# Softplus in one activation, and activation tables loaded by written-out instructions, in a two-model transformer kernel

## The chip, the cores and the metric

The kernel runs on one core of a Trainium2 chip. A core has TensorE (PE, matrix products), VectorE (DVE), ScalarE (ACT, activation functions by table), GpSimd (POOL) and SyncE (SP, which here issues the DMAs). The metric is the time of one execution on the device in microseconds (us); lower is better. Inputs, weights and output are float32 in HBM.

## The reference

Two models of two layers each run one after the other on x of 256 tokens by 1024. The first has a Fourier and convolution mixer, a windowed attention and two mixtures of experts. The second has, in each of its two layers, a SwiGLU feed-forward block, a mixer of three attentions (stick-breaking, MLA, NSA) and a second feed-forward block. What the change touches is the stick-breaking attention:

```python
z = jnp.einsum('bqhd,bkhd->...', qb, k).astype(jnp.float32) * scale
strict = kpos[None, :] < qpos[:, None]
log_one_minus = jnp.where(strict, -jax.nn.softplus(z), 0.0)
suffix = lax.cumsum(log_one_minus, axis=3, reverse=True) - log_one_minus
w = jnp.where(strict, jnp.exp(jax.nn.log_sigmoid(z) + suffix), 0.0)
o = jnp.einsum('bhqk,bkhd->bqhd', w, v)
```

softplus(z) is ln(1 + e^z), which is also max(z, 0) + ln(1 + e^-|z|). The rest that it touches is where ACT changes its table: RMS norm (square, sqrt) ahead of every block, SiLU in the feed-forward blocks and experts, the layer norm of the convolution (sqrt, then SiLU), the router's softmax (exp), and the sigmoids of the gates.

## The kernel before

Every engine has its own program, written out by hand as one function (tensor_program, scalar_program, vector_program, ...). Each runs its instructions strictly in order; between engines they wait on semaphores, in the code as events (E.sb_z, E.sb_pe, ...). All ACT operations go through the helper af in line 1314, all products through mm in line 671 and all turns (transposes) through tp in line 675, so the profile gives these lines for most operations. On DVE, line 1690 is a tensor-tensor operation, 1698 one with a scalar between two tensors, 1701 a copy, 1695 and 1694 a tensor with scalars.

Matrix products that need float32 accuracy are done in three products of a high and a low part: ACT copies the weights or activations to a rounded high part ("cut"), DVE subtracts to get the low part, PE multiplies. The weights come through a ring of 12 slots, of which 6 are lent out as working space (lent_r, ring) in the mixers and feed-forward blocks.

Eleven normalisations, number 0 to 10, run by normalise(u) on ACT and DVE: ACT squares token tile 0 with a running sum, DVE tile 1; DVE makes the mean (line 1695), ACT takes Sqrt of both, DVE the reciprocal (1753), ACT scales tile 0 and DVE tile 1, and PE turns the result. Numbers 5, 7, 8 and 10 stand ahead of the feed-forward blocks; there ACT goes on with the cut of half a weight tile and eight high-part copies of the turned activations, and DVE with the low parts; PE's products wait for these. Numbers 6 and 9 stand ahead of the mixers, 4 and 5 follow one another.

In a mixer, stage A weaves three streams on each engine in a fixed ratio: stick_breaking (eight heads in four pairs, n = 0 to 3), mla_prepare (norms, rotations and turns of the MLA heads) and fillers, products of hT with weights of w_in (128x512, four records of the trace to a step) that are not needed until later. For each pair n, PE makes the logits of two heads in PSUM banks 0 and 1 (128 keys on the partitions, 384 columns each), ACT and DVE make mx.sp = softplus(z) there, DVE masks it, PE adds up the suffix with triangular matrices in banks 2 and 3 and makes the logits of pair n+1, DVE adds the mask and writes mx.z, ACT takes the exponential in place, and PE multiplies it with the values ("pv"). Of softplus, ACT takes Abs, Exp(-x) and Ln(x + 1), each in place in mx.z, and DVE one operation max(z, 0) + mx.z.

ACT's functions come from tables. An instruction ACT_TABLE_LOAD changes the set; in the kernel before none is written in the code. The compiler puts one ahead of each function that the loaded set lacks. The wait on a semaphore is a part of the function's own instruction, so such a load stands ahead of the wait. Copy, Identity, Square and Abs need no change of table.

Of the kernel before, what the change touches and what calls it, by code (L numbers as in the profile page):

```python
# [15 lines left out]
P = 128  # L16
# [180 lines left out]
def build(nc, A, consts, n_col, n_row):  # L197
# [147 lines left out]
    mx = Space()  # L345
# [42 lines left out]
    class E:  # L388
# [87 lines left out]
                                  [("z", 0)] + [(s, m) for n in range(4) for s, m in (("suffix", n), ("z", n + 1), ("pv", n)) if m < 4]])  # L476
    E.sb_ln, E.sb_w = Event(nc, "sb_ln", keys(2, 4)), Event(nc, "sb_w", keys(2, 4))
    E.sb_sp, E.sb_add = Event(nc, "sb_softplus", keys(2, 4)), Event(nc, "sb_add", keys(2, 4))
# [833 lines left out]
    def scalar_program():  # L1312
# [37 lines left out]

        def normalise(u):
            if u:
                C.wait_ge(*E.x_new.at(u - 1))
            af(xn[:, 0, :], x[:, 0, :], ACT.Square, accum_out=stat[:, 0:1]).then_inc(*act.ev(E.norm_act, u, "sq"))
            C.wait_ge(*E.norm_dve.at(u, "mean"))
            af(stat[:, 2:4], stat[:, 2:4], ACT.Sqrt).then_inc(*act.ev(E.norm_act, u, "sqrt"))
            C.wait_ge(*E.norm_dve.at(u, "r"))
            af(xn[:, 0, :], x[:, 0, :], ACT.Copy, scale=stat[:, 4:5]).then_inc(*act.ev(E.norm_act, u, "x0"))

        def shifted_hT(u, mod_cols):  # L1360
# [13 lines left out]
        def fourier(ahead):  # L1374
# [25 lines left out]
            for _ in range(CONV_STEPS[0]):  # L1400
                next(ahead)
            C.wait_ge(*E.fc_dve.at(("var", 0)))
            af(fc.rstd, fc.rstd, ACT.Sqrt).then_inc(*act.ev(E.fc_act, ("std", 0)))
            C.wait_ge(*E.fc_dve.at(("norm", 0)))
            for ch in range(4):
# [9 lines left out]
        def experts(layer, ahead):  # L1415
            m, u = moe[layer], norm_of_moe[layer]
            normalise(u)
            for k in range(1, KT, 2):
                C.wait_ge(*E.hT_pe.at(u, k))
                C.wait_ge(*E.norm_dve.at(u, "r"))  # L1420
                af(hT[:, k, :], psum[:, k % 4, 0:S], ACT.Identity, scale=gain_col[:, k:k + 1],
                   bias=mods[1][:, k:k + 1]).then_inc(*act.ev(E.hT_act, u, k))
            C.wait_ge(*E.rt_dve.at(layer, "max"))
            af(m.aff, m.aff, ACT.Exp).then_inc(*act.ev(E.rt_act, layer, "exp"))
# [6 lines left out]
            for k in range(KT):  # L1431
                if k >= KT - ROUTER_STEPS[2]:
                    next(ahead, None)
                if k % 2:
                    C.wait_ge(*E.rt_pe.at(layer, ("gather", k)))
                    af(m.xg[:, 0:N_GRP, k, :], psum[:, k % 4, :].rearrange("p (g c) -> p g c", g=N_GRP), ACT.Identity,
                       scale=gain_col[:, k:k + 1], bias=mods[1][:, k:k + 1]).then_inc(*act.ev(E.rt_act, layer, ("xg", k)))
            run(ahead)
            for g in range(N_GRP):
                if g:  # L1440
                    C.wait_ge(*E.moe_dve.at(layer, g - 1, ("hid", 1)))
                C.wait_ge(*E.moe_mm.at(layer, g, "gate", 3, 3))
                for n in range(2):
                    half = slice(n * 512, (n + 1) * 512)
                    af(m.gated[:, half], psum[:, n, :], ACT.Silu).then_inc(*act.ev(E.moe_act, layer, g, ("silu", n)))
                C.wait_ge(*E.moe_mm.at(layer, g, "down", 3, 3))
                af(m.y[:, 0:512], psum[:, 6, :], ACT.Copy).then_inc(*act.ev(E.moe_act, layer, g, ("y", 0)))
# [78 lines left out]
        def stick_breaking(l):  # L1526
            for n in range(4):
                if n:
                    C.wait_ge(*E.sb_pe.at(l, "pv", n - 1))
                C.wait_ge(*E.sb_pe.at(l, "z", n))  # L1530
                af(mx.z, psum[:, 0:2, 0:3 * P], ACT.Abs).then_inc(*act.ev(E.sb_z, l, n))
                C.wait_ge(*act.now)
                af(mx.z, mx.z, ACT.Exp, scale=-1.0).then_inc(*act.own())
                C.wait_ge(*act.now)
                af(mx.z, mx.z, ACT.Ln, bias=1.0).then_inc(*act.ev(E.sb_ln, l, n))
                yield
                yield
                C.wait_ge(*E.sb_add.at(l, n))
                af(mx.z, mx.z, ACT.Exp).then_inc(*act.ev(E.sb_w, l, n))
                yield  # L1540

# [63 lines left out]
        def mixer(l):  # L1605
# [13 lines left out]
            for i2, (c0, width) in enumerate(mi_tokens):  # L1619
# [3 lines left out]
                dst = (mx.sv, mx.low)[i2][:, 1, :]  # L1623
                af(dst, psum[:, 2 * i2 + 1, 0:width], ACT.Copy).then_inc(*act.ev(E.mi_act, l, ("t", i2)))
            C.wait_ge(*E.mi_pe.at(l, "gates"))
            af(mx.gates, psum[:, 4, 0:48].rearrange("p (t n) -> p t n", t=TT), ACT.Sigmoid).then_inc(*act.ev(E.mi_act, l, "gates"))
# [27 lines left out]
            weave(fill, STEPS_C, (attention(nsa_units, 12 + 12 * l, bufs=mx.bufs), 1))  # L1654
            run(fill)
            cut("mo", l, 0, 0)
            for br in range(3):
# [30 lines left out]
    def vector_program():  # L1688
# [415 lines left out]
        def stick_breaking(l):  # L2104
            for n in range(4):
                yield
                V.wait_ge(*E.sb_ln.at(l, n))
                alone(stt(mx.sp, psum[:, 0:2, 0:3 * P], 0.0, mx.z, ALU.max, ALU.add))
                tt(mx.sp, mx.sp, wide(K("strict"), 2), ALU.mult).then_inc(*dve.ev(E.sb_sp, l, n))
                yield  # L2110
                V.wait_ge(*E.sb_pe.at(l, "suffix", n))
                tt(mx.z, psum[:, 2:4, 0:3 * P], wide(K("strict_add"), 2), ALU.add).then_inc(*dve.ev(E.sb_add, l, n))
                yield
# [291 lines left out]
```

## Time and profile before

| | us |
|---|---|
| median of 3 runs | 3107.53 |
| lowest, highest | 3103.37, 3108.70 |
| the profiled execution | 3107.78 |
| its span in the trace | 3106.4 |

In that execution PE is busy 2498.5 us (80% of the span), DVE 1141.0 us (37%), ACT 815.9 us (26%) and POOL 3.2 us. The mean clock granted to PE is 0.882 of full speed. The page also follows the chain of work that ended last back from the final instruction, and the trace lists single instructions in order of time. Times of an instruction are its start from the start of the span and its duration; idle time of its engine just before it stands in brackets, with what ended it. A granted clock of 1.00 is 2.4 GHz, 0.50 is 1.2 GHz.

### The profile page before, as it was taken

The numbers are of one execution on the slowest core, as the hardware profiler recorded it, in microseconds if no ns is written. First come the engines' busy times: TensorE is split into PE (matmuls) and PEld (weight loads), VectorE is DVE, ScalarE is ACT, GpSimd is POOL, SyncE is SP. The second block draws the span as 40 slices with busy tenths as digits, with TensorE's granted clock in tenths as the row PEclk, the third lists the DMA queues.
The fourth block names the chain that finished last, engine by engine and source line by source line (L and its number), as shares of the span: only waits on it lengthen the run. The fifth ranks groups of instructions, "written<-read, shape, count | busy, mean of one in ns | idle before, by whom it ended". The sixth has DMA issues, their size and how long they took to land.

```text
span 3106.4 us, 31572 instructions
## 1 busy us (share of the span) xinstructions
PE 2498.5 (80%) x13586; PEld 1587.9 (51%) x13586; DVE 1141.0 (37%) x1682; ACT 815.9 (26%) x1161; POOL 3.2 (0%) x7
## 2 busy tenths in 40 slices
PE   5877666667776666666998887889999998888899
PEld 2643111113552111113988453579989774545897
DVE  1732100103542100103545525465455543356554
ACT  2231000002240000002433332544444333224443
POOL 0000000000000000000000000000000000000000
PEclk9878888888877888888999888899999997899999
DMA  8468999997436999998654223246556432234463
GB/s 307 172 235 343 409 409 409 409 409 288 174 139 256 409 409 409 409 409 283 181 189 132 68 69 109 95 136 185 186 159 188 151 108 68 71 120 129 134 185 109
DMA packets 396960, 703.66 MB, mean 227 GB/s; under 512 B 17171, under 2 KB 232339, under 8 KB 396694
## 3 DMA queue, kind: packets, MB, share of 16 engines
q1 hardware_dynamic: 396822, 701.65, 63.7%
q8 instruction: 107, 1.75, 0.2%
q14 instruction: 31, 0.25, 0.0%
HBM read 700.56 MB, written 1.05 MB: 226 GB/s over the span
## 4 chain that ended last, share of the span: by engine, by line
PE 57%; DMA 24%; DVE 9%; ACT 6%; SPq 3%; issue 1%; DVEq 0%; ACTq 0%
PE psum L671 55%; DMA ring<-in_moe_w_down 10%; DMA ring<-in_moe_w_up 8%; DMA ring<-in_moe_w_gate 6%; SPq L548 3%; PE psum L675 2%; DVE arena L1698 2%; ACT ring L1314 1%; DVE arena L1690 1%; ACT L1314 1%; ACT lent_r L1314 1%; DVE lent_r L1690 1%; ACT xn L1314 1%; ACT arena L1314 1%; DVE xn L1690 1%
## 5 line engine op out<-in xcount | busy, mean ns | idle before, releaser
L671 PE MATMUL psum<-ring,arena 128*32 128x512 f32 (+3 forms) x3672 | 691.3, 686 | 293.9 <-DMA ring<-in_moe_w_up 111.1
L671 PE MATMUL psum<-lent_r 128*128 128x256 f32 (+1 forms) x3440 | 635.8, 298 | 25.5 <-DVE lent_r L1690 25.4
L671 PEld LDWEIGHTS psum<-ring,arena 128*32 128x32 f32 (+2 forms) x3672 | 188.9, 133 | 800.2 <-issue 285.7
L671 PEld LDWEIGHTS psum<-lent_r 128*128 128x128 f32 x3440 | 549.1, 194 | 45.6 <-issue 26.5
L671 PE MATMUL psum<-arena_r,lent_r 128*128 128x256 f32 (+1 forms) x1888 | 521.8, 318 | 16.2 <-DVE arena_r L1690 8.6
L1690 DVE TENSOR_TENSOR lent_r<-ring,lent_r 128x2048 fp32r<-128x2048 f32 (+1 forms) x158 | 349.3, 2212 | 283.2 <-ACT lent_r L1314 283.2
L671 PEld LDWEIGHTS psum<-arena_r,lent_r 128*128 128x128 f32 x1888 | 369.0, 196 | 40.5 <-DVE arena_r L1690 10.6
L1314 ACT ACTIVATE arena<-psum 128x512 f32<-128x512 f32 (+3 forms) x126 | 61.9, 507 | 1173.4 <-PE psum L671 1107.7
L1314 ACT ACTIVATE lent_r<-ring 128x2048 fp32r<-128x2048 f32 (+1 forms) x158 | 289.7, 1838 | 169.9 <-PE psum L671 169.9
L671 PE MATMUL psum<-ring,hT 128*128 128x512 f32 (+2 forms) x640 | 286.8, 586 | 5.2 <-ACT arena L1314 2.7
L1701 DVE COPY arena<-psum 128x256 f32<-128x256 f32 (+6 forms) x130 | 66.0, 512 | 482.6 <-PE psum L671 353.0
L671 PE MATMUL psum<-lent_r,arena_r 128*128 128x512 f32 x1056 | 241.5, 390 | 0.4 <-DVE lent_r L1690 0.2
L1701 DVE COPY arena<-arena 128x256 f32<-128x256 f32 (+3 forms) x32 | 13.0, 410 | 579.7 <-PE psum L671 577.4
L671 PEld LDWEIGHTS psum<-lent_r,arena_r 128*128 128x128 f32 x1056 | 197.6, 188 | 42.9 <-issue 2.0
L1314 ACT ACTIVATE ring<-psum 128x256 f32<-128x256 f32 (+3 forms) x172 | 81.1, 479 | 436.2 <-PE psum L671 399.4
L1690 DVE TENSOR_TENSOR arena_r<-ring,arena_r 128x256 fp32r<-128x256 f32 (+2 forms) x130 | 125.0, 963 | 138.4 <-ACT arena_r L1314 138.4
L671 PEld LDWEIGHTS psum<-ring,hT 128*128 128x128 f32 x640 | 118.2, 216 | 105.4 <-issue 95.4
L1314 ACT ACTIVATE arena_r<-ring 128x256 fp32r<-128x256 f32 (+2 forms) x130 | 109.7, 846 | 106.0 <-PE psum L671 62.7
L671 PE MATMUL psum<-arena_r 128*128 128x256 f32 (+2 forms) x704 | 117.3, 322 | 6.5 <-DVE arena_r L1690 6.5
L675 PE MATMUL psum<-const_sb,arena 128*128 128x128 f32 (+4 forms) x326 | 55.5, 311 | 68.8 <-DVE arena L1690 50.4
L671 PEld LDWEIGHTS psum<-arena_r 128*128 128x128 f32 x704 | 103.9, 199 | 13.4 <-DVE arena_r L1690 4.7
L671 PE MATMUL psum<-arena 128*64 128x128 f32 (+7 forms) x576 | 92.1, 391 | 18.6 <-DVE arena L1701 10.1
(127 smaller groups left out, 1487.7 us busy)
## 6 DMA issues: line engine op xcount, KB each, us to landing
ring<-in_moe_w_gate SPq DMA_DIRECT2D x128, 1024.0 KB, 18.5
ring<-in_moe_w_up SPq DMA_DIRECT2D x128, 1024.0 KB, 18.6
ring<-in_moe_w_down SPq DMA_DIRECT2D x128, 1024.0 KB, 18.5
ring<-in_ffn_wi SPq DMA_DIRECT2D x176, 512.0 KB, 5.2
ring<-in_ada_w SPq DMA_DIRECT2D x48, 1024.0 KB, 7.9
ring<-in_w_in SPq DMA_DIRECT2D x46, 1024.0 KB, 5.1
ring<-in_ffn_wo SPq DMA_DIRECT2D x44, 1024.0 KB, 4.9
ring<-in_w_out SPq DMA_DIRECT2D x8, 1024.0 KB, 5.0
```

The source lines that it names most:

```text
L548: Y.dma_start(view(ring_sb[:, n, :]), src).then_inc(slot_sem[n], 16)
L671: return T.matmul(out, lhsT, rhs, start=start, stop=stop, **kw)
L675: return T.transpose(out, in_, ident[0:k, 0:k])
L1314: return C.activation(out, a, f, **kw)
L1690: return V.tensor_tensor(out, a, b, op)
L1698: return V.scalar_tensor_tensor(out, a, s, b, op0, op1)
L1701: return V.tensor_copy(out, a)
```

## The change

In stick-breaking, Abs, Exp and Ln on ACT and the max-and-add on DVE become one activation, Softplus, which reads the logits from PSUM and writes mx.sp; DVE's mask then works on it at once. Softplus waits for the previous pair's suffix product (which reads mx.sp) in place of its pv product, and the addition on DVE that writes mx.z now waits for that pv. Behind Softplus stands a written-out load of Exp's table, and behind each exponential but the last one of Softplus's.

In every normalisation a load of Sqrt's table is written ahead of Square, and ahead of the wait for x. In those ahead of the feed-forward blocks a load of Silu's table follows the scaled copy. Further written-out loads: Sqrt and Silu at the convolution's norm, Exp at the router, Silu ahead of the experts, Sigmoid ahead of the mixer's gates and ahead of the merge of its three branches. The compiler still adds loads where a set is lacking; there are 73 in all against 70.

```diff
         def normalise(u):
+            C.preload_act_table(ACT.Sqrt)
             if u:
                 C.wait_ge(*E.x_new.at(u - 1))
             af(xn[:, 0, :], x[:, 0, :], ACT.Square, accum_out=stat[:, 0:1]).then_inc(*act.ev(E.norm_act, u, "sq"))
...
             af(xn[:, 0, :], x[:, 0, :], ACT.Copy, scale=stat[:, 4:5]).then_inc(*act.ev(E.norm_act, u, "x0"))
+            if u in norm_of_ff:
+                C.preload_act_table(ACT.Silu)
...
+            C.preload_act_table(ACT.Sqrt)
             C.wait_ge(*E.fc_dve.at(("var", 0)))
             af(fc.rstd, fc.rstd, ACT.Sqrt).then_inc(*act.ev(E.fc_act, ("std", 0)))
+            C.preload_act_table(ACT.Silu)
...
+            C.preload_act_table(ACT.Exp)
             C.wait_ge(*E.rt_dve.at(layer, "max"))
...
             run(ahead)
+            C.preload_act_table(ACT.Silu)
...
         def stick_breaking(l):
             for n in range(4):
+                C.wait_ge(*E.sb_pe.at(l, "z", n))
                 if n:
-                    C.wait_ge(*E.sb_pe.at(l, "pv", n - 1))
-                C.wait_ge(*E.sb_pe.at(l, "z", n))
-                af(mx.z, psum[:, 0:2, 0:3 * P], ACT.Abs).then_inc(*act.ev(E.sb_z, l, n))
-                C.wait_ge(*act.now)
-                af(mx.z, mx.z, ACT.Exp, scale=-1.0).then_inc(*act.own())
-                C.wait_ge(*act.now)
-                af(mx.z, mx.z, ACT.Ln, bias=1.0).then_inc(*act.ev(E.sb_ln, l, n))
+                    C.wait_ge(*E.sb_pe.at(l, "suffix", n - 1))
+                af(mx.sp, psum[:, 0:2, 0:3 * P], ACT.Softplus).then_inc(*act.ev(E.sb_z, l, n))
+                C.preload_act_table(ACT.Exp)
                 yield
                 yield
                 C.wait_ge(*E.sb_add.at(l, n))
                 af(mx.z, mx.z, ACT.Exp).then_inc(*act.ev(E.sb_w, l, n))
+                if n < 3:
+                    C.preload_act_table(ACT.Softplus)
                 yield
...
+            C.preload_act_table(ACT.Sigmoid)
             C.wait_ge(*E.mi_pe.at(l, "gates"))
...
             run(fill)
+            C.preload_act_table(ACT.Sigmoid)
             cut("mo", l, 0, 0)
...
         def stick_breaking(l):
             for n in range(4):
                 yield
-                V.wait_ge(*E.sb_ln.at(l, n))
-                alone(stt(mx.sp, psum[:, 0:2, 0:3 * P], 0.0, mx.z, ALU.max, ALU.add))
+                V.wait_ge(*E.sb_z.at(l, n))
                 tt(mx.sp, mx.sp, wide(K("strict"), 2), ALU.mult).then_inc(*dve.ev(E.sb_sp, l, n))
                 yield
                 V.wait_ge(*E.sb_pe.at(l, "suffix", n))
+                if n:
+                    V.wait_ge(*E.sb_pe.at(l, "pv", n - 1))
                 tt(mx.z, psum[:, 2:4, 0:3 * P], wide(K("strict_add"), 2), ALU.add).then_inc(*dve.ev(E.sb_add, l, n))
```

The orders of PE, POOL and SP stay as they are. On ACT, at pair n=2 of the first mixer (ring<-psum 128x768 is the read of the logits, arena or ring<-psum 128x512 the copy of a filler product; L1539 and L1545 are the two written-out loads in stick_breaking):

```order
 L1314 ACTIVATE arena<-psum 96x256 x3
 L1314 ACTIVATE arena<-psum 128x512
 L1314 ACTIVATE ring<-psum 128x768
-L1314 ACTIVATE ring<-ring 128x768
-L1314 ACT_TABLE_LOAD
-L1314 ACTIVATE ring<-ring 128x768
+L1539 ACT_TABLE_LOAD
 L1314 ACTIVATE arena<-psum 96x256
```

Two activations and the load between them leave, and a load for the exponential stands behind the Softplus; n=3 is built alike.

On ACT, from normalisation 4 to the first feed-forward block (xn,stat<-x is Square, stat<-stat Sqrt, xn<-x,stat the scaled copy, lent_r<-psum,col_sb the eight high-part copies, lent_r<-ring the cuts):

```order
+L1352 ACT_TABLE_LOAD
+L1314 ACTIVATE xn,stat<-x 128x1024
+L1314 ACTIVATE stat<-stat 128x2
+L1314 ACTIVATE xn<-x,stat 128x1024
+L1361 ACT_TABLE_LOAD
 L1314 ACTIVATE lent_r<-ring 128x1024
 L1314 ACTIVATE lent_r<-psum,col_sb 128x256 x8
 L1314 ACTIVATE lent_r<-ring 128x1024
 L1314 ACTIVATE lent_r<-ring 128x2048
-L1314 ACT_TABLE_LOAD
 L1314 ACTIVATE ring<-psum 128x256
```

Sqrt's load passes Square and the wait for x, and Silu's load passes three cuts and the eight copies.

On DVE, pair n=2 of the first mixer before (ring<-psum,ring is max-and-add, ring<-ring,const_sb the mask, ring<-psum,const_sb the sum into mx.z, arena<-psum 96x256 the copy of a turned MLA head):

```order
526 L1701 COPY arena<-psum 128x256 [waits s_sb_pe]
527 L1701 COPY arena<-psum 96x256 [waits s_mla_pe]
528 L1698 SCALAR_TENSOR_TENSOR ring<-psum,ring 128x768 [waits s_sb_ln]
529 L1690 TENSOR_TENSOR ring<-ring,const_sb 128x768 [waits s_own_dve]
530 L1690 TENSOR_TENSOR ring<-psum,const_sb 128x768 [waits s_sb_pe]
531 L1701 COPY arena<-psum 128x256 [waits s_sb_pe]
```

and after (lines are numbered anew):

```order
524 L1709 COPY arena<-psum 128x256 [waits s_sb_pe]
525 L1709 COPY arena<-psum 96x256 [waits s_mla_pe]
526 L1698 TENSOR_TENSOR ring<-ring,const_sb 128x768 [waits s_sb_z]
527 L1698 TENSOR_TENSOR ring<-psum,const_sb 128x768 [waits s_sb_pe]
528 L1709 COPY arena<-psum 128x256 [waits s_sb_pe]
529 L1698 TENSOR_TENSOR ring<-ring,const_sb 128x768 [waits s_sb_z]
```

The max-and-add is gone and the mask waits for ACT's Softplus itself; the copy ahead of it stays ahead.

## Rows read from the trace of the kernel before

**Rows 1.** The page: the chain that ended last, shares of the span.
```profile
PE 57%; DMA 24%; DVE 9%; ACT 6%; SPq 3%; issue 1%; DVEq 0%; ACTq 0%
```

**Rows 2.** ACT's groups: count | busy us, mean ns | idle before, releaser.
```profile
L1314 ACT ACT_TABLE_LOAD x70 | 89.8, 1283 | 14.8 <-DVE stat L2333 13.5
...
L1314 ACT ACTIVATE ring<-ring 128x768 f32<-128x768 f32 x24 | 20.2, 843 | 54.5 <-DVE ring L1690 54.1
```

**Rows 3.** Waits of PE, 1700 to 1850 us: total, times, longest.
```profile
PE psum L671 <- DVE ring L1690: 13.2, 4, 4.9
```

**Rows 4.** Timeline of ACT, n=3: start, duration [idle before].
```profile
1802.47 0.81 ACT L1314 ACTIVATE ring<-psum 128x768 f32<-128x768 f32 x1
1803.30 0.84 ACT L1314 ACTIVATE ring<-ring 128x768 f32<-128x768 f32 x1
1804.16 1.28 ACT L1314 ACT_TABLE_LOAD   x1
1805.46 0.84 ACT L1314 ACTIVATE ring<-ring 128x768 f32<-128x768 f32 x1
```

**Rows 5.** Timeline of DVE, n=2 (a copy) and n=3.
```profile
1788.28 0.42 DVE L1701 COPY arena<-psum 96x256 f32<-96x256 f32 x1 [4.08 <-PE psum L675]
...
1806.33 0.96 DVE L1698 SCALAR_TENSOR_TENSOR ring<-psum,ring 128x768 f32<-128x768 f32 x1 [5.83 <-ACT ring L1314]
1807.32 0.96 DVE L1690 TENSOR_TENSOR ring<-ring,const_sb 128x768 f32<-128x768 f32 x1
```

**Rows 6.** Timeline of PE, stage A of the first mixer (hT: fillers).
```profile
1732.20 0.70 PE L671 MATMUL psum<-ring 64*128 64x256 f32 x2 [3.05 <-DVE ring L1690]
...
1763.83 0.92 PE L671 MATMUL psum<-ring 64*128 64x256 f32 x2 [4.88 <-DVE ring L1690]
...
1788.29 1.88 PE L671 MATMUL psum<-ring,hT 128*128 128x512 f32 x4
1791.75 0.70 PE L671 MATMUL psum<-ring 64*128 64x256 f32 x2 [1.57 <-DVE ring L1690]
...
1796.37 0.93 PE L671 MATMUL psum<-ring 64*128 64x256 f32 x8
1797.23 1.98 PE L671 MATMUL psum<-ring,hT 128*128 128x512 f32 x4
...
1802.62 1.98 PE L671 MATMUL psum<-ring,hT 128*128 128x512 f32 x4 [0.69 <-ACT arena L1314]
1808.34 1.06 PE L671 MATMUL psum<-ring 64*128 64x256 f32 x2 [3.73 <-DVE ring L1690]
...
1816.38 3.08 PE L671 MATMUL psum<-ring,hT 128*128 128x512 f32 x4
```

**Rows 7.** Timeline of PE, n=2 in the second mixer.
```profile
2615.97 0.70 PE L671 MATMUL psum<-ring 64*128 64x256 f32 x2 [1.58 <-DVE ring L1690]
...
2624.63 3.51 PE L671 MATMUL psum<-ring,hT 128*128 128x512 f32 x4
```

**Rows 8.** Stretches: length, PE busy (count), granted clock, DMA share, GB/s.
```profile
1792.00:1796.00 4.00, 4.00 (x19) 1.00 0.00 0
...
2618.00:2622.00 4.00, 4.00 (x11) 0.50 0.00 0
```

**Rows 9.** Timeline of all engines, normalisation 7: mean, Sqrt, cut.
```profile
2076.47 0.17 DVE L1695 TENSOR_SCALAR stat<-stat 128x2 f32<-128x2 f32 x1
...
2077.67 0.20 ACT L1314 ACTIVATE stat<-stat 128x2 f32<-128x2 f32 x1
...
2079.16 1.04 ACT L1314 ACTIVATE lent_r<-ring 128x1024 fp32r<-128x1024 f32 x1
```

**Rows 10.** ACT: the group of Squares, and that of normalisation 1.
```profile
L1314 ACT ACTIVATE xn<-x 128x1024 f32<-128x1024 f32 x11 | 11.6, 1055 | 74.9 <-DVE x L1690 46.0 <-DVE x L1698 28.9
...
216.08 1.05 ACT L1314 ACTIVATE xn<-x 128x1024 f32<-128x1024 f32 x1
```

**Rows 11.** Timeline of ACT, Sigmoid's load at the first mixer's merge.
```profile
2001.60 1.28 ACT L1314 ACT_TABLE_LOAD   x1
```

More of the change, by code:

```diff
@@ L476, in build @@
                                   [("z", 0)] + [(s, m) for n in range(4) for s, m in (("suffix", n), ("z", n + 1), ("pv", n)) if m < 4]])
-    E.sb_ln, E.sb_w = Event(nc, "sb_ln", keys(2, 4)), Event(nc, "sb_w", keys(2, 4))
+    E.sb_w = Event(nc, "sb_w", keys(2, 4))
     E.sb_sp, E.sb_add = Event(nc, "sb_softplus", keys(2, 4)), Event(nc, "sb_add", keys(2, 4))
```

## Prediction

> **What bounds the kernel now.** I read the chain of work that ended last first: TensorE (PE) has 57% of it, weight transfers 24%, VectorE (DVE) 9% and ScalarE (ACT) 6% [rows 1]. So an ACT edit can only pay where PE waits for ACT, or for a DVE operation that ACT held up. Grouping ACT's instructions shows what is edited: 70 table loads of 1283 ns, and the in-place Exp and Ln on a 128x768 tile at 843 ns [rows 2]. The idle time ahead of these 70 loads is 14.8 us, 13.5 of it at the program's start: a load that the compiler placed sits right behind the previous ACT instruction and ahead of the wait of its user, so it already runs in ACT's idle time wherever there is any. Writing such a load out by hand gains nothing by itself; it pays only if it passes an instruction that is on the path.
>
> Two kinds of place are on the path. First the stick-breaking stage (stage A of each mixer, four head pairs n = 0 to 3, two layers). There PE waits 13.2 us in four waits for DVE's masked softplus [rows 3]: 3.05, 4.88, 1.57 and 3.73 us, and as much again in the second layer. Second the eleven normalisations, where the load of Sqrt stands between Square and Sqrt.
>
> **Stick-breaking, step by step.** For n=3 the old chain is a Copy of the filler product, Abs 0.80, Exp 0.84, load 1.28, Ln 0.84 [rows 4], then DVE's max-and-add and the mask, 0.99 us apart [rows 5], then PE. The new chain is Softplus and the mask. Softplus reads the same 128x768 of PSUM as Abs; no row shows it, so I bound it by Abs (0.80) and Ln (0.84) and take 0.80, since the functions in the rows differ only by where they read. Its own table is loaded behind the preceding exponential, which ended 4 us earlier, so the load is covered; without that cover it would cost 1.28. Removed from ACT and DVE: 0.84 + 1.28 + 0.84 + 0.99 = 3.95 us for each pair. PE takes only what it was waiting for, because it is filled with other products:
> - n=3: Softplus from 1802.47 to 1803.28, mask to 1804.27. PE is busy with a filler until 1802.62 + 1.98 = 1804.60 [rows 6]. The wait of 3.73 goes, gain 3.8.
> - n=2: the mask stands in DVE's queue behind the copy of a turned MLA key head that ends at 1788.70 [rows 5]; it would be done at 1789.7. PE's filler ends at 1788.29 + 1.88 = 1790.17, and PE restarted at 1791.75 [rows 6]. Gain 1.6.
> - n=0 and n=1: DVE comes to this pair only after long MLA work (squares and sums), so ACT's part is hidden anyway and what goes is the 0.99 us of max-and-add. For n=1 ACT's copies of turned heads also come about 1.7 us sooner (Exp and Ln gone, the load stays as that of Exp), of which PE's fillers leave 0.2. Gains 1.0 and 1.2; waits of about 2.1 and 3.9 us remain.
>
> That is 7.6 us a layer and 15.3 in both. The new DVE wait (the sum into mx.z waits for the previous pair's last product) and ACT's new wait for the previous suffix are for work finished at least 10 us earlier: nothing. The wasted loads (Exp behind Softplus when a Sqrt comes between, three more in all, 73 for 70) lie in ACT's idle time; if all three were exposed they would cost 3.8.
>
> **The clock behind those waits.** Suffix product and filler after n=2 in the first layer run at the high clock (2.4 GHz): PE starts at 1791.75, has the suffix done by 1796.37, and the filler takes 1.98. After n=3, behind a wait of 3.73, they run at the low one (1.2 GHz): 1808.34 to 1816.38 and 3.08 [rows 6]. In the second layer n=2 falls too: the same stretch that took 5.48 (1791.75 to 1797.23) takes 8.66 and its filler 3.51 [rows 7]; the granted clock is 0.50 there and 1.00 at n=2 of the first layer [rows 8]. If PE no longer stops ahead of n=2 and n=3, I expect both to stay high, as n=2 in the first layer did after 1.57 us: (8.04 - 4.62) + (3.08 - 1.98) = 4.5 for n=3 in each layer and 3.18 + 1.53 = 4.7 for n=2 in the second, 13.7 us together. The bounds are 0 (the clock falls all the same) and, if n=0 with its wait cut from 3.05 to 2.1 also stays high, another 4.7 or so in each layer, 23 in all. I take the middle: two of the three kinds of row have no wait left, n=0 keeps most of its own.
>
> **Normalisations.** In number 7, DVE's mean starts at 2076.47 and takes 0.17; Sqrt starts only at 2077.67, behind the load [rows 9]. With the load ahead of Square, in idle time (ACT waits 74.9 us in all ahead of the Squares [rows 10], in nine of the eleven), Sqrt starts at 2076.67: gain 1.0. It is the same for 6, 8, 9 and 10; in 2, 3 and 4 DVE's square is later and leaves 0.7, 0.9 and 0.9. Number 5 had no load (Sqrt's table is still in). In numbers 0 and 1 ACT goes from a Copy straight to Square, as number 1's row shows [rows 10], nothing covers the load, and Sqrt also waits for the mean behind it: +0.4 each. Against that, ahead of the four feed-forward blocks (5, 7, 8, 10) Silu's load now comes directly behind the scaled copy of x, ahead of the cut at 2079.16 and the eight high-part copies, through which the chain runs: +1.28 each. Before, that load lay behind them where PE was still multiplying. Sum: -5.0 - 2.5 + 0.8 + 5.1 = -1.6 us. Sigmoid's load at the merge moves from behind three copies to ahead of them in one unbroken run of ACT work [rows 11]: nothing. All other written-out loads stand where the compiler's did.
>
> The Trainium skill (ScalarE: Activation LUTs, What ACT_TABLE_LOAD costs) puts a switch at 1.28 for the load and about 1.38 for a drain. The trace disagrees: the next instruction starts 0.01 us behind the 1.28 [rows 4]. By the page the normalisations would come to about -2.5 instead of -1.6, the rest unchanged. The same page (Table sets: the hidden batching unit) advises to do all of one set before switching, which speaks against alternating Softplus and Exp. By it the eight pairs would lose up to a load each; the rows of ACT's idle time say the loads are covered.
>
> **Sum.** -15.3 - 13.7 - 1.6 = -30.6 us on the profiled execution of 3107.78 (span 3106.4), which lies 0.25 above the median of 3107.53: 3077 us.
>
> **Rivals.**
> 1. The clock falls all the same, or at other places in its stead. For: the second layer's n=2 fell after a wait of only 1.58 us. Against: n=2 of the first layer. Then -16.9: 3091. With one or two of the three stretches, 3082 to 3087.
> 2. The clock also stays high at n=0, in one or both layers: 3072 or 3067.
> 3. PE's fillers absorb more than I find, or loads of Softplus come out exposed ahead of their user, 1.28 in each of six places: about 3098 to 3103, near no change. Against it are the ends of the fillers, read above.
> 4. The loads do not move at all: then only the arithmetic counts and it is -15.3 with or without the clock, 3079 or 3092; inside the range.
> 5. Slower. Softplus is evaluated in several passes and takes D instead of 0.80. Its slack is 0.3 us at n=3, 2.4 at n=2, 1.1 at n=1 and over 10 at n=0, so it costs 3D - 6.2 a layer, and the waits return and with them the low clock. It turns the sign at D = 4.9 us, six times Abs; at 6 us the time would be 3114. Nothing in the rows shows a function that costs more than another.
>
> **Chances.** Forecast (3073 to 3081) 0.42; rival 2 0.17; rival 1 0.30; rival 3 0.06; rival 5 and anything else that makes it slower 0.05. The range takes in the forecast and rivals 1 and 2 but for their far ends: 3066 to 3094. Faster by over 0.2% (6 us, about what a measurement tells from no change) 0.91; within it 0.05; slower 0.04.
>
> **What would show it.** In stage A no ACT work but Softplus between a filler's Copy and DVE's mask; PE's waits for the softplus down from 13.2 us to about 6 a layer, at n=0 and n=1 alone; suffix products of n=2 and n=3 at 4.6 us each. In normalisation 7 Sqrt right behind the mean, and the cut a load later behind the scaled copy. It is wrong if Softplus takes over 1.1 us, if ACT stands at a load while DVE or PE waits for it, or if the granted clock in n=2 and n=3 is at 0.5.

## The result, and the profile after

| | before | after |
|---|---|---|
| median, us | 3108.11 | 3078.55 |
| lowest, highest | 3103.37, 3112.18 | 3076.59, 3084.10 |
| the profiled execution | 3107.78 | 3084.10 |
| its span | 3106.4 | 3082.8 |

The ratio of the times is 0.9908, with a 95% interval of 0.9889 to 0.9927: 29.6 us less. 3077 had been forecast. The profiled execution of after is the slowest of its four, so its trace shows a loss of 23.6 us in the span and not of 30; two further runs of the same kernel, with traces of their own, serve beside it below (the repeats of after). Before has four runs here, three in the table ahead of the change.

The page of after, first the busy time and then the chain that ended last, by engine (before: [rows 1]):

```profile
PE 2435.6 (79%) x13586; PEld 1573.0 (51%) x13586; DVE 1133.7 (37%) x1674; ACT 807.9 (26%) x1148; POOL 3.2 (0%) x7
...
PE 57%; DMA 26%; DVE 9%; ACT 5%; SPq 2%; issue 1%; DVEq 0%; ACTq 0%
```

ACT and DVE are busy only 8.0 and 7.3 us less; PE, with the same 13586 products, 62.9 us less, which fits the granted clock (0.882 before, 0.917 now). Most of that lies in the products of the experts, as their group in the page of after shows (count | busy us, mean ns | idle before, releaser):

```profile
L671 PE MATMUL psum<-ring,arena 128*32 128x512 f32 (+3 forms) x3672 | 646.1, 618 | 339.6 <-DMA ring<-in_moe_w_up 129.4
```

Before, the group was busy 691.3 us and idle 293.9: what the clock gave there, 45.2 us, went into waiting for weights, 45.7 us more. So the mean clock of a whole run is no measure of the gain: the two repeats of after have 0.919 and 0.900 at spans of 3075.9 and 3074.2 us.

The waits of PE in stage A of the first mixer of after, 1690 to 1840 us: total, times, longest (before: [rows 3], 13.2 us in four waits).

```profile
PE psum L671 <- DVE ring L1698: 5.9, 2, 3.8
```

The timeline of ACT at n=3 (before: [rows 4]): start, duration, operation, in brackets the idle time ahead and what ended it.

```profile
1798.73 0.81 ACT L1314 ACTIVATE ring<-psum 128x768 f32<-128x768 f32 x1
1799.56 1.28 ACT L1539 ACT_TABLE_LOAD   x1
```

The first row is Softplus. It takes 0.81 us, as Abs did in [rows 4], and no load stands ahead of it.

The timeline of PE in the same stage (before: [rows 6]). The pairs of 64x256 products open the suffix products of n=0, 1, 2 and 3; hT marks fillers.

```profile
1730.24 1.09 PE L671 MATMUL psum<-ring 64*128 64x256 f32 x2 [2.06 <-DVE ring L1698]
...
1762.39 1.22 PE L671 MATMUL psum<-ring 64*128 64x256 f32 x2 [3.85 <-DVE ring L1698]
...
1788.02 0.70 PE L671 MATMUL psum<-ring 64*128 64x256 f32 x2
...
1793.50 1.98 PE L671 MATMUL psum<-ring,hT 128*128 128x512 f32 x4
...
1798.89 1.98 PE L671 MATMUL psum<-ring,hT 128*128 128x512 f32 x4 [0.69 <-ACT arena L1314]
1800.80 0.70 PE L671 MATMUL psum<-ring 64*128 64x256 f32 x2
```

At n=2 and n=3 the wait is gone and the pair takes 0.70 us, which is the high clock; at n=0 and n=1 waits of 2.06 and 3.85 us remain, and the pair takes 1.09 and 1.22.

Normalisation 7, timeline of DVE (the mean) and ACT (before: [rows 9]):

```profile
2065.91 0.17 DVE L1703 TENSOR_SCALAR stat<-stat 128x2 f32<-128x2 f32 x1
...
2066.12 0.20 ACT L1314 ACTIVATE stat<-stat 128x2 f32<-128x2 f32 x1 [0.32 <-DVE stat L1703]
2066.55 1.15 ACT L1314 ACTIVATE xn<-x,stat 128x1024 f32<-128x1024 f32 x1 [0.23 <-DVE stat L1761]
2067.72 1.28 ACT L1361 ACT_TABLE_LOAD   x1
2069.01 1.06 ACT L1314 ACTIVATE lent_r<-ring 128x1024 fp32r<-128x1024 f32 x1
```

Sqrt now starts 0.21 us behind the start of the mean (before 1.20), and the cut 2.46 us behind that of the scaled copy, since Silu's load stands between them.

Because PE's instructions are the same in both kernels, they can be laid side by side one by one. How much shorter (-) or longer (+) a stretch between two of them is than in before; the first column gives its bounds on before's clock, and a normalisation's stretch starts with the last product ahead of it:

| stretch, us | after | first repeat of after | second repeat |
|---|---|---|---|
| norms 4 and 5 and first products, 1439 to 1480 | +0.5 | +0.4 | +0.4 |
| stage A, first mixer, 1700 to 1840 | -11.4 | -15.3 | -15.3 |
| norm 7 and first products, 2074 to 2100 | +0.6 | +1.7 | +1.7 |
| norm 8 and first products, 2272 to 2300 | +0.2 | +0.8 | +0.9 |
| stage A, second mixer, 2530 to 2670 | -14.9 | -15.9 | -15.9 |
| norm 10 and first products, 2903 to 2960 | +0.1 | +1.3 | +1.3 |
| whole span | -23.6 | -30.5 | -32.2 |

The gain is that of the two stages A. It was forecast at 12.1 and 16.9 there.

### The profile page after: what moved, and what is told of

Its sections match the earlier page's. It is cut to its first block, busy times and chain, and to the rows that moved or that the text cites. A ratio compares the mean times of both kernels' runs of the same rounds, so it can differ in the third digit from the quotient of the medians.

```text
span 3082.8 us, 31557 instructions
## 1 busy us (share of the span) xinstructions
PE 2435.6 (79%) x13586; PEld 1573.0 (51%) x13586; DVE 1133.7 (37%) x1674; ACT 807.9 (26%) x1148; POOL 3.2 (0%) x7
## 4 chain that ended last, share of the span: by engine, by line
PE 57%; DMA 26%; DVE 9%; ACT 5%; SPq 2%; issue 1%; DVEq 0%; ACTq 0%
PE psum L671 55%; DMA ring<-in_moe_w_up 10%; DMA ring<-in_moe_w_down 8%; DMA ring<-in_moe_w_gate 7%; PE psum L675 2%; SPq L548 2%; DVE arena L1706 2%; DVE arena L1698 2%; ACT ring L1314 1%; ACT lent_r L1314 1%; DVE lent_r L1698 1%; ACT arena L1314 1%; DVE arena L1709 1%; DVE xn L1698 1%; DVE arena_r L1698 1%
## 5 line engine op out<-in xcount | busy, mean ns | idle before, releaser
L671 PE MATMUL psum<-ring,arena 128*32 128x512 f32 (+3 forms) x3672 | 646.1, 618 | 339.6 <-DMA ring<-in_moe_w_up 129.4
L671 PE MATMUL psum<-lent_r 128*128 128x256 f32 (+1 forms) x3440 | 637.2, 299 | 25.7 <-DVE lent_r L1698 25.7
```

What stands on the lines that cost most here:

```text
L671: return T.matmul(out, lhsT, rhs, start=start, stop=stop, **kw)
```

## The experiments

Each run of a set stands beside runs of the kernel before on the same chip (medians 3110.59, 3108.01 and 3107.96 in the three sets). The sets ran on different chips, so across sets the ratios are to be compared, not the times.

**Which half of the change does it.** One kernel has the stick-breaking part alone, the other the written-out loads alone. The first drops these lines from after, and the five further loads outside stick-breaking likewise:

```diff
         def normalise(u):
-            C.preload_act_table(ACT.Sqrt)
...
-            if u in norm_of_ff:
-                C.preload_act_table(ACT.Silu)
```

> The changed kernel without its written-out loads outside stick-breaking: the compiler places those again (Sqrt's behind Square, Silu's behind the cuts). My theory puts nearly the whole gain into stick-breaking, about 26 us by the trace of the changed kernel (11.3 in the first mixer, 14.5 in the second), and the moved loads at -1.6: this kernel at 3080 +- 3 us, Sqrt of normalisation 7 again 1.0 us later, cut 1.28 earlier relative to the scaled copy. The rival, that the loads carry the gain, expects over 3095.

Measured: 3076.47 us (3075.44 to 3077.29), ratio 0.9892 [0.9877, 0.9907], 0.5 below the 3080 +- 3 expected and far from the rival.

The second keeps all those loads and puts the old softplus back:

```diff
-                af(mx.sp, psum[:, 0:2, 0:3 * P], ACT.Softplus).then_inc(*act.ev(E.sb_z, l, n))
-                C.preload_act_table(ACT.Exp)
+                af(mx.z, psum[:, 0:2, 0:3 * P], ACT.Abs).then_inc(*act.ev(E.sb_z, l, n))
+                C.wait_ge(*act.now)
+                af(mx.z, mx.z, ACT.Exp, scale=-1.0).then_inc(*act.own())
+                C.wait_ge(*act.now)
+                af(mx.z, mx.z, ACT.Ln, bias=1.0).then_inc(*act.ev(E.sb_ln, l, n))
```

> The other part alone: all written-out loads outside stick-breaking, with Abs, Exp, Ln and max-and-add as before. My theory: -1.6 us, 3106 +- 3, not to be told from no change. The rival: 3095 or below. A second rival, that the Silu load in front of the cuts costs more than the 1.28 counted, expects over 3110.

Measured: 3109.15 us (3106.23 to 3114.64), ratio 1.0 [0.9992, 1.0009], at the upper end of the 3106 +- 3 expected. The whole gain is stick-breaking's, and the loads together are worth nothing that can be measured. That is a sum of a gain and a cost, though, as the next kernel shows.

The trace of this second kernel holds a lesson on the clock. Its instructions at n=2 of the first mixer, and their wait, are those of before, but the timeline of PE reads:

```profile
1786.12 0.70 PE L671 MATMUL psum<-ring 64*128 64x256 f32 x2 [1.58 <-DVE ring L1699]
1788.99 1.22 PE L671 MATMUL psum<-ring 64*128 64x256 f32 x2
1793.16 1.66 PE L671 MATMUL psum<-ring 64*128 64x256 f32 x8
```

In before the eight products behind the same wait took 0.93 us [rows 6], here 1.66: the clock falls during the suffix. After a wait of 1.6 us it may fall or not with the same instructions around it, which is also what [rows 6] against [rows 7] showed.

**Silu's load.** After without the load of Silu in the four normalisations ahead of the feed-forward blocks:

```diff
-            if u in norm_of_ff:
-                C.preload_act_table(ACT.Silu)
```

> The changed kernel without the written-out load of Silu in the four normalisations ahead of the feed-forward blocks; the compiler places it again behind the cuts. My theory: the cut in normalisation 7 starts 1.28 us sooner behind the scaled copy, and so do PE's first products, 5.1 us in all: 3073.5 +- 3. The rival, that PE or DVE would be late there anyway, expects the time of the changed kernel, 3078.5.

Measured: 3069.07 us (3066.52 to 3071.96), ratio 0.9869 [0.9856, 0.9882]. That is 4.4 below the 3073.5 expected and 9.5 below after as measured in its own set (12 by the ratios), more than four loads. But in the same set it is also 7.4 us below the kernel with stick-breaking alone (3076.47, with no overlap of the runs), from which it differs by the written-out loads other than Silu's in the normalisations. The prediction had put -6.7 on that difference, all of it Sqrt's. So Sqrt's loads do gain, and Silu's give it back. The kernel was run again, together with after.

> The changed kernel once more, as one corner of a two by two square: Silu's load written out or not, and the masks of n=0 and n=1 as they are or earlier. 3073 to 3079.

> The changed kernel without Silu's load in the four normalisations. If the first run's gain is real (a load of 1.28 us on the path in each of four places, plus a little), it is 5 to 8 us below the changed kernel of the same set; if that was the spread between chips and runs, 0 to 3.

Measured: after 3074.08 us (3071.56 to 3079.51), ratio 0.9892 [0.9875, 0.991]; without Silu's load 3069.23 us (3068.27 to 3070.05), ratio 0.9874 [0.9859, 0.9889]. The difference is 4.9 us, near the 5.1 of four loads and at the lower end of the 5 to 8 expected. Timeline of PE in normalisation 10, first of before, then of after's second repeat, then of the kernel without Silu's load; the rows are the two groups of turns.

```profile
2908.37 1.97 PE L675 MATMUL psum<-const_sb,xn 128*128 128x128 f32 x8 [4.86 <-ACT xn L1314]
2910.97 1.97 PE L675 MATMUL psum<-const_sb,xn 128*128 128x128 f32 x8 [0.64 <-DVE arena_r L1698]
```

```profile
2873.91 1.97 PE L675 MATMUL psum<-const_sb,xn 128*128 128x128 f32 x8 [3.87 <-ACT xn L1314]
2877.94 1.97 PE L675 MATMUL psum<-const_sb,xn 128*128 128x128 f32 x8 [2.06 <-DVE arena_r L1706]
```

```profile
2870.67 1.97 PE L675 MATMUL psum<-const_sb,xn 128*128 128x128 f32 x8 [3.87 <-ACT xn L1314]
2873.27 1.97 PE L675 MATMUL psum<-const_sb,xn 128*128 128x128 f32 x8 [0.64 <-DVE arena_r L1704]
```

Both effects reach PE. Sqrt's load ahead of Square takes 0.99 us off the wait for the first turns, and Silu's load puts 1.42 us on the wait for the second, since DVE's low parts there wait for what ACT does behind the load. It is the same 1.42 in normalisations 5, 7 and 8. Over the stretches of the table above, the kernel without Silu's load has -1.8, -0.2, -0.2 and -1.0 us at normalisations 5, 7, 8 and 10, where after's second repeat has +0.4, +1.7, +0.9 and +1.3: 7.5 us in all, 5.7 of them the four waits, the rest products that run at the low clock for longer behind them.

The two profiled spans differ by 5.5 us and not by 7.5, because the clock also falls at other places that the edit doesn't touch. Without the load stage A of the second mixer is 3.0 us shorter than in the repeat (-18.9 against -15.9), stage A of the first 2.8 us longer (-12.5 against -15.3), and the turns and products just ahead of normalisation 7 take 2.5 us more. Timeline of PE at n=0 of the second mixer, after's second repeat first:

```profile
2540.11 0.70 PE L671 MATMUL psum<-ring 64*128 64x256 f32 x2 [2.06 <-DVE ring L1698]
2542.42 1.17 PE L671 MATMUL psum<-ring 64*128 64x256 f32 x2
2546.54 1.66 PE L671 MATMUL psum<-ring 64*128 64x256 f32 x8
```

```profile
2540.00 0.70 PE L671 MATMUL psum<-ring 64*128 64x256 f32 x2 [2.06 <-DVE ring L1696]
2542.31 0.70 PE L671 MATMUL psum<-ring 64*128 64x256 f32 x2
2544.62 0.93 PE L671 MATMUL psum<-ring 64*128 64x256 f32 x8
```

The same wait of 2.06 us stands ahead of both. In one the clock falls within the suffix, in the other it stays high throughout, which is rival 2 of the prediction in one place. The profiled run of after lost it at once (1730.24 above, 1.09 us), which accounts for most of its 4 us more in the first mixer.

**Does a wait that PE gets back cost more than its length?** Four more reads of the logits ahead of Softplus at n=2 and n=3 hold it up; their results are overwritten by it.

```diff
+                if n >= 2:
+                    for _ in range(4):
+                        af(mx.sp, psum[:, 0:2, 0:3 * P], ACT.Abs).then_inc(*act.own())
+                        C.wait_ge(*act.now)
                 af(mx.sp, psum[:, 0:2, 0:3 * P], ACT.Softplus).then_inc(*act.ev(E.sb_z, l, n))
```

> The changed kernel with four Abs (0.80 us each, 3.3 us together) put ahead of Softplus at n=2 and n=3, into the same tile, so that PE's waits come back there in part: about 0.9 us at n=2 and 3.0 at n=3, in both mixers, 7.8 us by their lengths. If a wait also brings the low clock with it, as I reckoned, suffix and filler behind n=3 (and perhaps n=2) cost 4.5 us more each: 17 to 26 us in all, 3095 to 3104. If the clock gain has another cause, only the 7.8: 3086.

Measured: 3112.08 us (3107.44 to 3121.84), ratio 1.0015 [1.0004, 1.0026]: 33.5 above after (33 by the ratios), beyond the range expected. The timeline of ACT at n=2 and that of PE show why:

```profile
1776.90 3.33 ACT L1314 ACTIVATE ring<-psum 128x768 f32<-128x768 f32 x4
1780.26 1.28 ACT L1314 ACT_TABLE_LOAD   x1
```

```profile
1783.40 0.86 PE L671 MATMUL psum<-ring 64*128 64x256 f32 x2 [3.62 <-DVE ring L1702]
...
1808.29 1.22 PE L671 MATMUL psum<-ring 64*128 64x256 f32 x2 [5.78 <-DVE ring L1702]
```

The text ahead of the prediction has Abs among the functions that need no change of table, since it needed none in the kernel before. Beside Softplus it does: the compiler put a load ahead of the four and another behind them, 2.56 us more in each pair than meant, and the waits that came back are 3.62 and 5.78 us in each mixer, 18.8 in both. The other 14.7 us I put down to the clock and what follows from it; the next kernel tests that. (The Trainium skill, ScalarE: Activation LUTs, Table sets: the hidden batching unit, lists abs among the cheap functions of every set; the loads of this trace say otherwise for the set that is loaded for Softplus.)

The same with Copy, which needs no load:

```diff
-                        af(mx.sp, psum[:, 0:2, 0:3 * P], ACT.Abs).then_inc(*act.own())
+                        af(mx.sp, psum[:, 0:2, 0:3 * P], ACT.Copy).then_inc(*act.own())
```

> The changed kernel once more, beside the others on one chip. 3078 +- 3 us.

> As the run with four Abs ahead of Softplus at n=2 and n=3, but with four Copies, for which Softplus's table serves (Abs brought two loads of 1.28 with it and waits of 3.6 and 5.8 us, 18.8 in both mixers, at a price of 33.5). Waits of 0.9 at n=2 and 3.0 at n=3, 7.8 us in all. If the low clock comes with a wait, 4.5 more at n=3 in each mixer, and at n=2 where it falls there: 17 to 26 us above the changed kernel; 7.8 if not.

Measured: after 3073.45 us (3068.82 to 3077.26), ratio 0.9889 [0.9875, 0.9904]; with the Copies 3094.37 us (3089.78 to 3099.44), ratio 0.9957 [0.9944, 0.997]. After is 1.6 below the 3078 +- 3 expected of it. The price of the Copies is 20.9 us, within the 17 to 26. PE's waits for the softplus, 1685 to 1830 us of the kernel with the Copies, and its timeline at n=2 and n=3:

```profile
PE psum L671 <- DVE ring L1702: 9.9, 4, 3.9
```

```profile
1785.73 0.70 PE L671 MATMUL psum<-ring 64*128 64x256 f32 x2 [0.92 <-DVE ring L1702]
1788.04 0.70 PE L671 MATMUL psum<-ring 64*128 64x256 f32 x2
1790.35 0.93 PE L671 MATMUL psum<-ring 64*128 64x256 f32 x8
...
1801.66 0.70 PE L671 MATMUL psum<-ring 64*128 64x256 f32 x2 [3.08 <-DVE ring L1702]
1805.02 1.22 PE L671 MATMUL psum<-ring 64*128 64x256 f32 x2
1809.06 3.62 PE L671 MATMUL psum<-ring,hT 128*128 128x512 f32 x4
```

Waits of 0.92 and 3.08 us came back, 8.0 in both mixers, at a price of 20.9. After 0.92 the clock stays high; after 3.08 it falls in the middle of the suffix, and the filler behind it takes 3.62 us in place of 1.98. By the traces the two stages A together are 17.3 us longer than in the first repeat of after: 7.6 of it PE's idle time, and 9.7 the same products taking longer, 9.3 of these behind n=3 (4.6 and 4.7, for the 4.5 expected). So the two parts of the forecast are both real. The last 3.6 of the 20.9 us lie outside these stages and aren't explained.

**The two waits that are left.** At n=0 and n=1 DVE comes to the mask late because of MLA work ahead of it. Here the mask of n=0 is moved ahead of the squares of the q norm, and that of n=1 ahead of the copy of the fifth turned q head:

```diff
+MASK_AT = {2: 0, 9: 1}
...
+        def mask(l, n):
+            V.wait_ge(*E.sb_z.at(l, n))
+            tt(mx.sp, mx.sp, wide(K("strict"), 2), ALU.mult).then_inc(*dve.ev(E.sb_sp, l, n))
...
-                V.wait_ge(*E.sb_z.at(l, n))
-                tt(mx.sp, mx.sp, wide(K("strict"), 2), ALU.mult).then_inc(*dve.ev(E.sb_sp, l, n))
+                if n >= 2:
+                    mask(l, n)
...
+            def mla_and_masks():
+                for step in itertools.count():
+                    if step in MASK_AT:
+                        mask(l, MASK_AT[step])
+                    if next(mla, mla) is mla:
+                        return
+                    yield
```

> The changed kernel with DVE's masks of n=0 and n=1 moved ahead in its queue: n=0 to before the squares of the q norm, n=1 to before the copy of the fifth turned q head, both behind Softplus's end in the trace. My theory (PE's wait and, behind it, the low clock set the price): the waits of 2.06 and 3.85 us go; the suffix and the fillers behind them run at the high clock, 8 us a layer at n=0 and, with DVE's norm of k becoming the bound, 4 to 6 at n=1: 24 to 28 us in all, 3050 to 3056. The rival, that only the waits count, expects 11.8: 3067. A third, that DVE's MLA work is the bound of stage A, so that moving a mask frees nothing, expects 3078.

Measured: 3051.27 us (3043.04 to 3053.34), ratio 0.9817 [0.9804, 0.983], 22.2 below after in the same set. PE's longest waits, 1685 to 1830 us, and its timeline from n=0 (the 128x256 rows are pv products, the 64x256 rows suffixes):

```profile
PE psum L672 <- ACT ring L1315: 4.8, 4, 2.8
```

```profile
1727.17 0.93 PE L672 MATMUL psum<-ring 64*128 64x256 f32 x8
...
1734.57 0.88 PE L672 MATMUL psum<-ring 128*64 128x256 f32 x8 [2.84 <-ACT ring L1315]
...
1744.48 0.70 PE L672 MATMUL psum<-ring 64*128 64x256 f32 x2
...
1755.15 0.88 PE L672 MATMUL psum<-ring 128*64 128x256 f32 x8 [1.50 <-ACT ring L1315]
```

The 5.9 us a mixer of waiting for the softplus are gone; all four suffixes run at 0.70 and 0.93 us. What is late next is the exponential, which pv waits for: 4.8 us in four waits, most of it there before (3.3 in after). In the profiled run of the third set, below, PE is idle 7.5 us less in the two stages than in after's second repeat (11.8 gone, part of it come back as waits for the exponential), and the same products take 16.5 us less, 11.6 of them at n=1. So most of the 22 us is the clock's. It is less than the 24 to 28 expected, as a difference.

**Everything at once.** Masks early, without Silu's load, and Sqrt's load written out only from normalisation 2 on (in 0 and 1 nothing covers it):

```diff
-            C.preload_act_table(ACT.Sqrt)
+            if u >= 2:
+                C.preload_act_table(ACT.Sqrt)
```

> The kernel with the early masks, without Silu's load ahead of the cuts, and without Sqrt's load ahead of Square in normalisations 0 and 1. My theory: another 5.1 + 0.8 us by the lengths of the loads (9 by the run without Silu's load): 3042 to 3050.

Measured: 3050.44 us (3044.91 to 3051.12), ratio 0.9812 [0.9799, 0.9825]. That is 0.4 above the 3042 to 3050 expected, and against 3051.27 in the same set no gain, where 5.9 had been expected. To see whether Silu's load counts at all on this base, the two were run without the change to Sqrt's load, beside after and after without Silu's load:

> The changed kernel with the masks of n=0 and n=1 earlier on DVE: 22 to 26 below the changed kernel of the same set, as in its first run.

> Both edits. The load and the masks lie in different stages, so if the two are independent it is as much below the kernel with the early masks as the version without Silu's load is below the changed kernel: 5 to 8 us, 3043 to 3046. If what a sooner start of the feed-forward products gives is taken back behind them (a clock that falls elsewhere), it is within 3 us of the kernel with the early masks.

Measured: masks early 3053.31 us (3052.98 to 3054.94), ratio 0.9824 [0.9809, 0.9839]; the same without Silu's load 3044.85 us (3042.39 to 3051.08), ratio 0.9795 [0.9779, 0.981]. With masks early the time is 20.8 us below after, where 22 to 26 had been expected; leaving out Silu's load as well takes off 8.5 more, just over the 5 to 8. The square of the third set:

| us | masks as in after | masks early |
|---|---|---|
| Silu's load written out | 3074.08 | 3053.31 |
| left to the compiler | 3069.23 | 3044.85 |

Both edits hold in both rows and columns, and the last kernel, 63 us under the kernel before, is the fastest by its median. The size of the small one stays uncertain, though: 4.9 and 8.5 here, 0.8 between the two kernels of the second set, and 2.5 between the profiled runs of the right column. There the four normalisations gain 7.1 us together; stage A, which differs in nothing, is 1.5 us shorter in the first mixer and 1.8 longer in the second, and between the first mixer's stage A and normalisation 7 it loses 3.7. Whether Sqrt's load in normalisations 0 and 1 matters can't be told from the times at that spread. In the traces PE's first turn of normalisation 1 comes 0.42 us later with the load than without.

## Why the prediction was right, point by point

**Softplus** takes 0.81 us, where 0.80 had been taken from Abs. Its load and that of Exp lie in ACT's idle time. Rival 5 (several passes) falls with this row, and rival 4 (the loads don't move) too.

**The waits.** Forecast: 13.2 us a layer down to about 6, with 2.1 and 3.9 left at n=0 and n=1. Measured: 5.9, with 2.06 and 3.85. The method was to end each wait at the later of DVE's mask and PE's filler; it was right to 0.1 us at all four pairs, and so rival 3 falls. PE's idle time ahead of and between the four suffixes falls by 1.0, 1.2, 1.6 and 3.7 us, for 1.0, 1.2, 1.6 and 3.8 forecast. Of 15.3 us in both layers 14.6 are left in the repeats, because a wait of 0.2 us for the exponential of n=3, which the prediction doesn't have, is new in each, and the rest is rounding.

**The clock.** Forecast -13.7, with bounds 0 and -23. The stages A are shorter by 26.3 us in the profiled run and by 31.2 in its repeats. PE's idle time there is 12.4 and 14.6 us less, so the same products take 13.8 and 16.6 us less. The time of PE's products, idle time left out, from one suffix to the next (for n=3 up to 1840 and 2670 us of before):

| us | before | after | both repeats | with the Copies |
|---|---|---|---|---|
| first mixer, n=0 | 23.7 | 25.5 | 20.8 | 20.8 |
| n=1 | 25.7 | 24.9 | 25.3 | 25.4 |
| n=2 | 12.2 | 12.1 | 12.1 | 12.2 |
| n=3 | 31.2 | 26.6 | 26.6 | 31.2 |
| second mixer, n=0 | 23.8 | 25.5 | 24.0 | 24.0 |
| n=1 | 24.4 | 25.0 | 25.1 | 25.2 |
| n=2 | 16.9 | 12.1 | 12.1 | 12.2 |
| n=3 | 32.0 | 27.3 | 27.3 | 32.0 |

The three stretches that the prediction named (n=3 twice, n=2 in the second mixer) gained 4.6, 4.7 and 4.8 us in all three traces of after, 14.1 for 13.7, and the Copies took n=3 back to what it was, behind a wait of 3.08 us; that shows the mechanism. Two things differ from the forecast in detail. First n=0 doesn't simply keep its state: with 2.06 us ahead of it, it ran fully at the high clock, fell in its middle, or fell at its start, from run to run, worth up to 4 us a mixer. Second, the prediction gave n=2 of the first layer no gain from the clock since in that one trace it ran high; the experiment with the loads alone found it low behind the same wait. Rows of one trace told the price of a fallen clock well, but not how often it falls. That before's one trace had n=2 high in one mixer and low in the other, and not twice low, is luck for the sum: with both low, as with the loads alone, it would have been 4.7 us more.

**Normalisations.** Forecast -1.6 for Sqrt's and Silu's loads together. The times agree with a sum near zero and can't tell its sign: stick-breaking alone has the ratio 0.9892, after 0.9908, 0.9889 and 0.9892 in its three sets, and the loads alone lie within 2.8 us up and 2.5 down. The two terms behind the sum were both right. Sqrt's loads were put at -6.7. Counted from the last product ahead of a normalisation, PE's first turn comes 0.99 us sooner than in before at numbers 6 to 10, 0.7 and 0.9 at 2 and 3, 0.9 for 4 (at the turns of 5), and 0.4 later at 1, in all three traces of after; with number 0, where 0.4 later is seen on ACT, that is the forecast term by term, and the time says 7.4 us in the first set. Silu's loads were put at +5.1; each costs PE 1.42 us and not 1.28, 5.7 in all, and the time says 4.9 on after. What the prediction lacked is that the products behind the turns start at the low clock and leave it sooner or later from run to run: at normalisation 7 the three traces have +0.6, +1.7 and +1.7 where the two terms give +0.4. The prediction's own signs didn't fit together, either: ACT standing at a load while DVE waits was to mean that it is wrong, and this is just what its term for Silu's load describes. (Of what the order ahead of the prediction marks as new there, Square, Sqrt and the scaled copy are in both kernels; ACT has 16 activations fewer and 3 loads more, 1148 rows for 1161.)

The Trainium skill's drain of about 1.38 us (ScalarE: Activation LUTs, What ACT_TABLE_LOAD costs) isn't there in after either: the cut follows the 1.28 us load of 2067.72 by 0.01 us. The -2.5 that the prediction worked out for it doesn't come out: with 1.38 us more for each moved load, an estimate, the eight normalisations that gain would gain 11.0 more and the four of Silu's load lose 5.5 more (at 0 and 1 the two cancel), -7.1. The Trainium skill's advice to do all of one set before switching (the same page, Table sets: the hidden batching unit) would have counted against the change; the alternation of Softplus and Exp cost nothing here, since the waits that are left are those worked out without any load in them.

**The sum** held because its parts did: 14.6 for 15.3 of waits, 13.8 to 16.6 for 13.7 of clock, and near zero for 1.6. The trace on record is 6.9 and 8.6 us longer than its siblings, 4.9 of it in the stages A, where n=0 fell at its start, so it alone would have suggested a miss that wasn't there.

## What to carry to other kernels

Removing a chain of small operations from ScalarE and VectorE pays only where TensorE waits for it, and there it may pay twice: 8.0 us of waits put back cost 20.9, because waits of 3 us let the clock fall under the products that follow (about half of it by the traces). End each wait by hand at the later of its producer and of TensorE's own fillers, and then look at which engine's queue holds the rest; here two masks moved ahead of other VectorE work brought 22 us, nearly as much as the whole change. Don't write out a table load that the compiler already places ahead of a wait, and never put one ahead of instructions that the next stage waits for (1.42 us at PE each). Do write one out where the compiler's stands inside a chain that TensorE waits for and there is idle time ahead of the chain: Sqrt's, moved ahead of Square, brought up to 0.99 us each. And start a comparison of a stretch at the last product ahead of the edit, or changes of the clock from elsewhere hide its effect.

## What the runs showed of the hardware

- Softplus over 128x768 from PSUM takes 0.81 us on ScalarE, as Abs and Copy do (3.33 us for four Abs, 4.17 for four Copies and a Softplus).
- Abs and Softplus aren't in one set: the alternation cost two loads of 1.28 us a pair. Copy needed none.
- A wait of 0.92 us left TensorE's clock high (0.70 us for the pair of products); 3.08 let it fall within 3.6 us of the restart in both mixers (1.22 for the pair); 2.06 and 1.58 did either, in runs of one kernel or with the same instructions around. Length alone doesn't decide it: behind the wait of 2.84 us for the exponential at n=0 of the first mixer the next filler took 1.98 us in after, where the suffix ahead had been at the low clock, and 3.21 and 3.44 in its repeats, where it had been at the high one.
- Such falls make two runs of one kernel differ by up to 4 us in a stage that has no difference in its code, which is more than a table load on the path is worth.
- The next activation follows a table load of 1.28 us by 0.01 us.
